# Two-part products in a gate/up stage: high and low matmuls alternated tile by tile, and the order around the stage moved

## The reference, cut to what matters

```python
h = rmsnorm_2(x, g_pre_ffn[l]) * (1.0 + sc_f) + sh_f
f = (jax.nn.silu(h @ w_gate[l]) * (h @ w_up[l])) @ w_down[l]
x = x + gt_f * rmsnorm_2(f, g_post_ffn[l])
```

## Time and profile before

| | |
|---|---|
| median of 3 runs | 3111.51 us (3109.59 to 3114.95) |
| the profiled execution | 3109.59 us, span of its instructions 3107.9 us |
| PE busy | 3061.8 us, 99% of the span |
| DVE, ACT, POOL busy | 2162.9, 1158.2, 345.0 us |
| gate/up stage, products of `fast_pair` | from 1797.86 to 2619.07 us |
| down stage | from 2619.07 to about 3098 us |

### The profile page before, as it was taken

How to read it: one execution, slowest core, us unless ns; L and a number is a source line. 1 busy time by engine, 2 the same in 40 slices (tenths; PEclk the granted TensorE clock), 3 DMA queues, 4 the chain that set the end, 5 groups by cost and what they waited for, 6 DMA issues and landing times.

```text
span 3107.9 us, 41800 instructions
## 1 busy us (share of the span) xinstructions
PE 3061.8 (99%) x15416; PEld 2566.8 (83%) x15416; DVE 2162.9 (70%) x2827; ACT 1158.2 (37%) x1522; POOL 345.0 (11%) x505
## 2 busy tenths in 40 slices
PE   8999999999999999999999899999999999999998
PEld 7888877888878888888888688888888888888887
DVE  6666656868885444555688888888888887666665
ACT  5323343213233333444532354444444444222223
POOL 0111100111100000000011300000000000112113
PEclk9999999999999999999999899999999999999999
DMA  4444454875762222222277356666666666555544
GB/s 189 146 129 128 129 196 161 314 267 216 263 248 82 82 81 81 82 82 81 102 278 259 147 162 176 175 175 174 175 174 173 176 175 210 176 190 176 195 171 163
DMA packets 118267, 525.00 MB, mean 169 GB/s; under 512 B 22081, under 2 KB 22353, under 8 KB 80913
## 3 DMA queue, kind: packets, MB, share of 16 engines
q1 hardware_dynamic: 63920, 321.15, 29.3%
q0 software_dynamic: 50352, 174.40, 19.2%
q10 hardware_dynamic: 3888, 28.03, 2.3%
HBM read 435.17 MB, written 37.76 MB: 152 GB/s over the span
## 4 chain that ended last, share of the span: by engine, by line
PE 96%; DVE 3%; DMA 0%; ACT 0%; DVEq 0%; issue 0%; ACTq 0%
PE PS L1723 17%; PE PS L1305 15%; PE PS L1307 15%; PE PS L1306 15%; PE PS L1727 9%; PE PS L1755 5%; PE PS L1754 5%; PE PS L1756 5%; PE PS L1574 1%; PE PS L1601 1%; PE PS L1358 1%; PE PS L1360 1%; PE PS L1359 1%; PE PS L1589 1%; PE PS L1471 0%; PE PS L1430 0%
## 5 line engine op out<-in xcount | busy, mean ns | idle before, releaser
L1305 PE MATMUL PS<-XHL,WH 128*128 128x512 f32 x1968 | 775.3, 394 | 5.2 <-DVE WL L1766 2.1
L1307 PE MATMUL PS<-XHL,WL 128*128 128x512 f32 x1968 | 766.2, 389 | 0.0
L1306 PE MATMUL PS<-XHL,WH 128*128 128x512 f32 x1968 | 766.0, 389 | 0.0
L812 ACT ACTIVATE WH<-RAW 128x2048 fp32r<-128x2048 f32 x138 | 263.9, 1912 | 521.1 <-PE PS L1307 513.1
L1305 PEld LDWEIGHTS PS<-XHL,WH 128*128 128x128 f32 x1968 | 369.4, 188 | 93.5 <-issue 10.7
L1307 PEld LDWEIGHTS PS<-XHL,WL 128*128 128x128 f32 x1968 | 369.4, 188 | 77.7
L1306 PEld LDWEIGHTS PS<-XHL,WH 128*128 128x128 f32 x1968 | 369.6, 188 | 77.0 <-issue 2.2
L1766 DVE TENSOR_TENSOR WL<-RAW,WH 128x2048 fp32r<-128x2048 f32 x138 | 316.5, 2294 | 80.1 <-ACT WH L812 80.0
L1150 ACT ACTIVATE QH<-RAW 128x1024 fp32r<-128x1024 f32 x210 | 222.6, 1060 | 256.1 <-PE PS L1727 251.6
L2593 DVE TENSOR_TENSOR QL<-RAW,QH 128x1024 fp32r<-128x1024 f32 x210 | 256.6, 1223 | 60.4 <-ACT QH L1150 60.2
L1754 PE MATMUL PS<-WH,FH 128*128 128x512 f32 x704 | 273.9, 389 | 0.0
(11 more groups left out here) (371 smaller groups left out, 4378.1 us busy)
## 6 DMA issues: line engine op xcount, KB each, us to landing
RAW<-w_units_dram SPq DMA_DIRECT2D x268, 1024.0 KB, 4.8
ADA<-w_ada_dram POOLq DMA_DIRECT2D x192, 512.0 KB, 5.6
SUM<-RAW POOLq DMA_DIRECT2D x42, 512.0 KB, 4.6
RAW<-SUM POOLq DMA_DIRECT2D x42, 512.0 KB, 4.5
FR<-f_dram SPq DMA_DIRECT2D x10, 1024.0 KB, 5.5
spill_dram<-SIG POOLq DMA_DIRECT2D x24, 256.0 KB, 2.3
f_dram<-TMP SPq DMA_DIRECT2D x22, 256.0 KB, 7.1
f_dram<-FO SPq DMA_DIRECT2D x22, 256.0 KB, 6.8
```

What stands on the lines that cost most here:

```text
L812: act.activation(WH[:, slot, :], RAW[:, slot, :], ACT.Copy).then_inc(hi_ready, 1)
L1305: pe.matmul(PS[:, bank, :], wh, rh[:, x, :], start=k == 0, stop=False)
L1306: pe.matmul(PS[:, bank, :], wh, rl[:, x, :], start=False, stop=False)
L1307: ins = pe.matmul(PS[:, bank, :], wl, rh[:, x, :], start=False, stop=k == n - 1)
```

## The change

TensorE's `fast_pair` no longer runs eight high and then eight low matmuls: it alternates, for each k the high one and then the low one. The wait on `q_hi` is gone, and the wait on `q_lo` stands at the head of the product. On DVE, `plain_hidden(1)` and its drain move ahead of low part 1 and `sum_1`, and low part 3 moves behind the operations on `TC`. In the down stage `hidden_lo(1, 0)` moves ahead of the first `down_read`. On SP the save of hidden tile 43 moves ahead of the load of chunk 1, and that load also waits until tile 43 is made.

```diff
@@ sync
             down_load(1)
+            hidden_saved(FF_TILES - 1, f_d[FF_TILES - 1], 1)
             for n in range(2, FF_TILES):
                 if n % 4 == 2 and n // 4 + 1 < FF_CHUNKS:
                     c = n // 4 + 1
                     if c == 1:
                         sp.wait_ge(q_done, Q0 + PRODUCTS * FAST)
+                        sp.wait_ge(f_made, FF_TILES)
                     sp.wait_ge(x_ready, X_HID + FF_CHUNK * c)
                     hidden_loaded(c)
-                    if c == 1:
-                        hidden_saved(FF_TILES - 1, f_d[FF_TILES - 1], 1)
@@ tensor, fast_pair
-                    pe.wait_ge(q_hi, PRODUCTS * s + (j + 1))
+                    pe.wait_ge(q_lo, q + j + 1)
...
                     for k in range(FULL_K):
-                        pe.matmul(in_halves(PS[:, bank, :]), QH[:, slot, k * P:(k + 1) * P], fast_data(j, k),
-                                  start=k == 0 and j not in (3, 5, 6), stop=False, skip_group_check=True)
-                    pe.wait_ge(q_lo, q + j + 1)
-                    for k in range(FULL_K):
-                        ins = pe.matmul(PS[:, bank, 0:HALF_S], QL[:, slot, k * P:(k + 1) * P], fast_data(j, k)[:, HIGH.get(j, 0), :],
-                                        start=False, stop=k == FULL_K - 1, skip_group_check=True)
+                        wh, wl = (w[:, slot, k * P:(k + 1) * P] for w in (QH, QL))
+                        x = fast_data(j, k)
+                        pe.matmul(in_halves(PS[:, bank, :]), wh, x, start=k == 0 and j not in (3, 5, 6), stop=False,
+                                  skip_group_check=True)
+                        ins = pe.matmul(PS[:, bank, 0:HALF_S], wl, x[:, HIGH.get(j, 0), :], start=False, stop=k == FULL_K - 1,
+                                        skip_group_check=True)
                     ins.then_inc(q_done, 1)
@@ vector, way in
             lo_part(0, 0, 0, 0)
+            plain_hidden(1)
+            v.drain().then_inc(copied, 1)
             lo_part(0, 0, 1, 1)
             sum_1(0)
-            plain_hidden(1)
-            v.drain().then_inc(copied, 1)
             lo_part(0, 0, 2, 2)
-            lo_part(0, 0, 3, 3)
             v.wait_ge(t_hi, 3)
...
             ins.then_inc(t_lo, 1)
+            lo_part(0, 0, 3, 3)
             lo_part(0, 0, 4, 0)
@@ vector, down stage
-                if 1 <= n and c + 1 < FF_CHUNKS:
+                if c + 1 < FF_CHUNKS:
                     hidden_lo(c + 1, m)
...
                     down_read(c, 4 * m + b)
-                    if n == 0 and b == 2:
-                        hidden_lo(1, 0)
```

## The result

The changed kernel takes 3130.16 us (median; 3128.41 to 3134.07), against 3111.51 before. The forecast was 3110.0 with a range to 3128, so it missed on the slow side. (An execution of the kernel before that took 3516.07 us counts as slow and is left out.)

A forecast was written before the change was run, and what follows sets the result against it. TensorE was taken to bound the kernel; alternating -5.9, way in +2.4 and way out +2.0 us summed to -1.5 us, 3108.1 profiled or 3110.0 us as median. The range was 3092 to 3128.

The forecast's parts named there:

- TensorE sets the end: From 1797.86 us on, every microsecond TensorE's sequence gains or loses, or newly stalls, moves the end by a microsecond.
- Alternating, -5.9 us: In the product stage, alternating high and low matmuls makes each pair 2.5 ns cheaper, over 2352 pairs 5.9 us gained.
- the middle that the rows offer twice: Cost taken for an alternated high and low pair in the product stage: 346.7 ns, between bounds of 340.0 and 355.
- the two sums: Two ways to price an alternated pair, 226.7 + 120 ns or 233 + 113.3 ns, both given as 346.7.
- recovery is paid at every k: Rival: each high matmul behind a low one pays recovery, 352 ns a pair; +11.1 us with the ends, 3122.6; chance 0.34.
- both kinds at their streaming rate: Rival: alternated high matmuls fall to 226.7 ns, low ones to 113.3; -17.2 us with the ends, 3094.3; chance 0.2.
- One load under way, which must fit under the matmul ahead: On TensorE in the product stage, one weight load runs per matmul and must fit under the matmul before it.
- The wait on the low part, 0: Moving this wait to a product's head, 1.84 us earlier, costs nothing amid the stage: low parts are 3.8 us early.
- The way in, +2.4 us: At the product stage's start, reordered DVE work makes products 2, 3 and 6 late: 2.4 us lost, 1.5 to 3.5.
- The way out, +2.0 us: At the down stage's start, chunk 1's later load delays low part, first bank read and group 4: 2.0 us, 0.7 to 3.3.
- The sum: Whole kernel: -5.9 + 2.4 + 2.0 = -1.5 us, 3108.1 profiled, 3110.0 as median.
- worst pair: Dearest alternated pair allowed for in the product stage: 355 ns, 13.6 us lost; with the ends +18.0, 3129.5, cut to 3128.

The follow-up runs named there:

- wide_low: Kernel before with high and low matmuls alternated and each low matmul widened from 256 to 512 columns; 3355.43 us in one execution.
- halves: Kernel before, still eight high and eight low, with each high matmul split into two of 256 columns; 3136.76 us in one execution.
- group2: Kernel before with the low-part wait at each product's head and matmuls alternating in groups of two high, two low; 3109.55 us in one execution.
- head_wait: Kernel before with only the low-part wait moved to each product's head and the high-part wait gone; 3111.62 us in one execution.
- ends_only: Changed kernel with TensorE's matmuls put back to eight high then eight low; 3120.14 us against 3112.27 before, ratio 1.0027.
- load_late: Kernel before with SP's part of the change alone: hidden tile 43 saved first, chunk 1's load behind it; 3112.30 us in one execution.

## Why the prediction was wrong, point by point

- **TensorE sets the end.** Right for the traced executions. What its starts from 1797.86 on show, 18.65 us, is the difference of the spans but for the 2.15 us from earlier. The two executions near 3114 us have no trace to look at.
- **Alternating, -5.9 us.** Wrong, and the main failure: +9.8, inside the bounds given (340 to 355 ns) and near the dear one. The step that failed is "the middle that the rows offer twice", 346.7 ns a pair. In its place the runs show 353.3: a high matmul costs 236.4 ns, more than the 226.7 and than the 233 of the two sums, and a low one 116.9. Both sums paired a high matmul's distance in one surrounding with a low one's in another, and the second, 233 + 113.3, is 346.3 and rests on a 113.3 that was no row but half of another. Pairing them so works where a matmul's cost is its own, and it isn't here: `wide_low` and `halves` show even costs for one size alone, every mixture costs more than their sum of 346.7, and how much more depends on the order.
- **The rival "recovery is paid at every k".** Nearest of all, with 352 ns for 353.3; its +11.1 us fell short of 18.65 by 3.1 in the rate and 4.4 at the ends. Of its mechanism one half holds: the high ones get dearer with every return, 230.1 ns in runs of eight, 236.4 alone. The other half, low ones that stay at 120, doesn't: they fell to 116.9, and in `group2` to 115.2, where the pair is cheaper than before. So the price of a return can't be read off the high ones. Strict alternation, one by one, is the dearest order tried throughout the stage.
- **The rival "both kinds at their streaming rate".** Out, by every run. The low ones did get cheaper (116.9), the high ones lost more, and even by themselves 256 columns take 120.0 ns and not 113.3 (`halves`). By the Trainium skill ("TensorE: Matmul & The Clock Gate", "Step-by-step: what each phase is for") the weight load for the next matmul steals nothing from the one that runs. The traces agree that the load goes beside the matmul ahead: amid the stage each one starts 1 to 6 ns behind the start of that matmul, in every order tried. But 353.3 against 346.7 ns shows that hidden loads don't make each kind run at its own rate.
- **One load under way, which must fit under the matmul ahead.** The first half agrees with the traces. The second isn't shown: a load's row lasts 186 to 193 ns in every order, and low matmuls stand 120 ns apart all the same.
- **The wait on the low part, 0.** Right (`head_wait`).
- **The way in, +2.4 us.** Right: 2.4 in the changed kernel, 2.6 in `ends_only`, late at products 2, 3 and 6 as said, with 0.45, 1.38, 0.44 us for the 0.25, 1.5, 0.6 worked out. That the sum fits so well is in part luck, as the three errors cancel.
- **The way out, +2.0 us.** The chain was right, link by link; its size was not. The term that was mis-sized is the load's latency, 7.1 us taken and 9.7 measured, beyond the 8.4 that I held for the worst (8.8 in `load_late` and `ends_only`). More left with it: the next weight loads stand 0.44 us behind it on SP (2637.56), where they stood 3.35 us behind before (2622.62), and the engines moved 3.2 MB while it was under way (331 GB/s over 9.66 us) against 1.7 MB (295 over 5.7). No run separates that from other causes, and the busy share of the DMA engines doesn't tell the loads apart: 0.93, against 0.92 beside the load that took 5.8 us and 1.01 beside the one that took 8.4. And a cost was missing: behind this gap of 4.56 us TensorE's clock was at its lower level for eight matmuls, 1.6 us more.
- **The sum.** -5.9 became +9.8 and +2.0 became +6.4: 20.1 us, which is the miss (3130.2 - 3110.0). The range ended at 3128 because the worst rate was cut and the ends had been given no room of their own in it; worst pair and worst ends together were 3132.

Left open: what mechanism in TensorE makes the cost of a mixture. The distances repeat in fixed sequences, such as the period of three pairs in the alternated order, which looks like starts that fall into and out of step with something that both kinds share; that is a guess, and no run here tests it. Open too: what the two executions of the changed kernel near 3114 us did otherwise.

## What to carry to other kernels

A matmul's cost in one surrounding is no price for it in another: where an edit changes who stands beside whom at a rate of thousands, treat the bounds as the forecast until a short run has measured the pattern, and don't alternate sizes one by one: here runs of two, four and eight were all cheaper. Before moving an instruction ahead of others on an engine, ask both when its input lands now and whether the same edit moves that landing: two edits, each free, made a wait together. Price a load that moves by the slowest one seen at that place and with room beyond it, not by the middle (5.8, 8.4, 8.8 and 9.7 us here), and a stall of some microseconds on TensorE by the clock behind it as well.

## What the runs showed that I had not expected

- Matmuls of this type, each with a weight load ahead, stand 226.7 ns apart with 512 columns alone (`wide_low`, down stage) and 120.0 with 256 alone (`halves`). Mixed, a pair of them costs 348.3 (runs of two), 349.2 (eight), 350.8 (four) or 353.3 ns (one), not in order of run length: the high ones get dearer as runs get shorter, and the low ones cheaper, but not in step.
- Alternated one by one, the distances repeat every three pairs (1.060 us), within 1 ns and across products, which have eight pairs each.
- After 3.67 us without a matmul the clock stayed at its upper level (`ends_only`); after 4.56 us it was at the lower one for eight distances (changed kernel). One case of each.
